# An attention kernel in float32: P·V as three products of split operands, and block 1's query blocks in rising order

## What is computed

```python
# block 1, two layers, 16 meta tokens ahead of the 1024; 8 heads of 64, one shared k and v
s = einsum('bqhd,bkd->bqhk', q_idx, k_idx)                  # index scores
score = einsum('bqhk,bqh->bqk', relu(s), w_idx * idx_scale)
score = where(visible, score, NEG_INF)
_, sel = lax.top_k(score, 256)                              # 256 keys per query
logits = einsum('bqhd,bqkd->bqhk', q, k[sel]) * attn_scale
p = softmax(where(valid, logits, NEG_INF))
attn = einsum('bqhk,bqkd->bqhd', p, v[sel])
y_a = einsum('bte,ed->btd', attn * silu(gate_a), w_a)
# block 2, one layer
y_na  = neighbourhood_attention(qa, ka, va, rpb) @ w_branch_na    # 8 heads, 8 x 16 window on a 16 x 64 grid
y_swa = windowed_gqa_with_sink(qb, kb, vb, sink) @ w_branch_swa   # 8 query heads, 2 kv heads, |i-j| <= 128
```

## Time and profile before

| | |
|---|---|
| median of 3 runs | 3604.36 us (3599.98 to 3604.37) |
| profiled execution | 3597.27 us, span 3595.4 us |
| TensorE busy | 3357.2 us, 93% |
| VectorE, ScalarE, GpSimd busy | 50%, 35%, 34% |
| mean granted TensorE clock | 0.973 |
| DMA | 230.59 MB, 64 GB/s |

### The profile page before, as it was taken

The page is one execution under the profiler, slowest core; times in us unless marked ns, Lnnn a source line. Parts: engine busy times, 40 slices in busy tenths (PEclk is TensorE's granted clock), DMA queues, the critical chain, the costliest instruction groups (busy, mean ns, idle before and its releaser), DMA issues. The chain is left out here.

```text
span 3595.4 us, 45087 instructions
## 1 busy us (share of the span) xinstructions
PE 3357.2 (93%) x18148; PEld 2932.0 (82%) x18148; DVE 1806.4 (50%) x3015; ACT 1261.4 (35%) x1894; POOL 1212.1 (34%) x835
## 2 busy tenths in 40 slices
PE   5899999998998999999898999998899899999997
PEld 4788999998888899999875788876777588888885
DVE  4578999653356799975424144433433411000014
ACT  4553212452265422135314344344522522222223
POOL 3324633215332363311434432311253432323331
PEclk8999999999999999999998999999999999999998
DMA  5101122204310112210322411111242111111111
GB/s 139 33 24 42 57 81 90 76 1 160 101 54 24 36 51 78 93 72 1 124 90 82 127 40 35 40 47 48 71 141 94 30 47 47 47 47 49 46 52 48
DMA packets 284175, 230.59 MB, mean 64 GB/s; under 512 B 31473, under 2 KB 257408, under 8 KB 283584
## 3 DMA queue, kind: packets, MB, share of 16 engines
q1 hardware_dynamic: 253792, 116.40, 12.0%
q0 software_dynamic: 23264, 85.89, 6.8%
q10 hardware_dynamic: 6912, 25.41, 1.8%
HBM read 177.29 MB, written 52.36 MB: 64 GB/s over the span
## 5 line engine op out<-in xcount | busy, mean ns | idle before, releaser
L548 PE MATMUL big<-H,wsp 128*128 128x348 f32 (+2 forms) x9792 | 1916.6, 355 | 70.6 <-POOL H L1605 33.9
L548 PEld LDWEIGHTS big<-H,wsp 128*128 128x128 f32 (+1 forms) x9792 | 1684.7, 190 | 271.8 <-issue 35.5
L1605 POOL TENSOR_TENSOR wsp<-raw,wsp 128x1024 fp32r<-128x1024 f32 (+2 forms) x246 | 544.0, 2211 | 1488.2 <-ACT wsp L1071 1478.1
L548 PE MATMUL big<-SP,wsp 128*128 128x512 f32 x1920 | 451.0, 395 | 0.0
L548 PEld LDWEIGHTS big<-SP,wsp 128*128 128x128 f32 x1920 | 359.1, 187 | 90.4 <-issue 1.7
L1071 ACT ACTIVATE wsp<-raw 128x1024 fp32r<-128x1024 f32 (+2 forms) x246 | 238.4, 969 | 509.0 <-PE big L548 372.0
L2263 DVE MAX8 top<-SC 128x8 f32<-128x272 f32 (+6 forms) x448 | 367.9, 821 | 0.0
L2269 DVE MATCH_REPLACE8 SC<-top,SC 128x272 f32<-128x272 f32 (+6 forms) x448 | 364.5, 814 | 0.0
L2422 DVE TENSOR_TENSOR X<-X,big 128x1024 f32<-128x1024 f32 (+1 forms) x26 | 29.6, 1139 | 476.1 <-PE big L548 475.9
L1119 ACT ACTIVATE rows_a<-rows_a,head_min 128x1040 f32<-128x1040 f32 (+8 forms) x130 | 101.9, 784 | 128.1 <-DVE head_min L2041 127.9
L697 PE MATMUL small<-V,PT_a 128*128 128x64 f32 x1152 | 146.4, 272 | 0.1
(11 more groups left out here) (268 smaller groups left out, 3828.3 us busy)
## 6 DMA issues: line engine op xcount, KB each, us to landing
raw<-in_w_in SPq DMA_DIRECT2D x108, 512.0 KB, 3.9
raw<-in_w_ff SPq DMA_DIRECT2D x64, 512.0 KB, 4.1
raw<-in_w_out SPq DMA_DIRECT2D x24, 512.0 KB, 5.3
gate_b_scratch<-tm POOLq DMA_DIRECT2D x16, 522.0 KB, 3.1
gate_a_scratch<-tm ACTq DMA_DIRECT2D x16, 522.0 KB, 2.9
tm<-gate_a_scratch POOLq DMA_DIRECT2D x16, 522.0 KB, 3.8
tm<-gate_b_scratch POOLq DMA_DIRECT2D x16, 522.0 KB, 4.6
tm<-xT_scratch POOLq DMA_DIRECT2D x16, 522.0 KB, 5.2
```

The costliest lines, as they stand in the source:

```text
L548: mm = pe.matmul(dst(o, width), w[wp][:, k, 0:cols], rhs(xp, k)[:, t0:t0 + width], start=(k == 0 and i == 0), stop=(k == rows - 1 and i == 2))
L1605: pool.tensor_tensor(dst, src, hi.bitcast(F32), ALU.subtract).then_inc(*S.inc(name, *key))
```

## The change

- P and V are split for their product. `V` and `V2` are float32r with a high and a low part; ScalarE copies the high part, VectorE subtracts for the low one (`values_lo`). `PT_a` and `PT_b` too: `move_hi` copies all tiles of a unit on ScalarE, `move_lo` subtracts on VectorE. `values` makes three products per tile: with P high those by both parts of V, for all tiles, then P low by V high.
- The transposes have two PSUM banks (`tiles_a`, `tiles_b`); where a unit has up to four tiles the banks alternate, else it is cut in two groups. Scores of 576 keys stand in one area of two banks, of which there is one instead of two; masks are one instruction each.
- TensorE makes the scores of unit k ahead of the transposes of k-2, VectorE the mask ahead of the move, and ScalarE the move of unit k-2 ahead of the exponent of unit k-1 (before: of unit k), and what runs beside (`between`) last.
- Block 1's query blocks run from 0 up to 7, with three row buffers in `tm`; silu gates are loaded block by block. The meta queries are left out in the last layer (`LAST_A`).
- The index stage leaves out query block 0, whose keys are all visible: `qi` has 896 columns in two pieces of 448.

```diff
+        V = sb("V", [P, 2, NQ, HD], F32R)
+        V_meta = sb("V_meta", [P, HD])
         SC = sb("SC", [P, SCORE_COLS])
...
-            for j in range(NQ - 1, -1, -1):
+            for j in range(NQ):
...
-        BLOCKS_A = [*range(NQ - 1, -1, -1), -1]
+        LAST_A = [-1] * (DEPTH - 1) + [NQ - 1]
+        BLOCKS_A = [*range(NQ), -1]
...
+        def tiles_a(u, k):
+            if u["tiles"] > 4:
+                return [(0, 0, 4), (1, 4, u["tiles"] - 4)]
+            return [(k % 2, 0, u["tiles"])]
...
+        def row_a(k):
+            return tm[:, (2, 3, 0)[k % 3], 0:1040]
...
+        def tiles_b(u, k):
+            if len(u["kts"]) > 4:
+                return [(0, 0, 3), (1, 3, len(u["kts"]) - 3)]
+            return [(k % 2, 0, len(u["kts"]))]
...
+        def logits_b(u, k):
+            at = k % 2 * BANK if u["key"][0] == "s" else 0
+            return big[0][:, at:at + u["n"]]
...
-                        pe.wait_ge(*S.at("masked", *units[k - 2]["key"]))
-                    near = min(u["n"], BANK)
+                    back = 2 if u["key"][0] == "s" else 1
+                    if k >= back:
+                        pe.wait_ge(*S.at("masked", *units[k - back]["key"]))
+                    at = logits_b(u, k)
                     for part in range(2):
...
                 def transposes(k):
                     u = units[k]
                     pe.wait_ge(*S.at("exped", *u["key"]))
-                    if k:
-                        for e in moved_events(units[k - 1]):
-                            pe.wait_ge(*S.at(*e))
-                    for kt, _, _ in u["kts"]:
-                        at = place(u, kt) * P
-                        mm = pe.transpose(big[1][:, at:at + P], rows_b[:, k % 4, kt * P:(kt + 1) * P], ident[:])
-                    mm.then_inc(*S.inc("turned", *u["key"]))
+                    for i, (bank, first, count) in enumerate(tiles_b(u, k)):
+                        if bank in bank_free:
+                            pe.wait_ge(*S.at(*bank_free[bank]))
+                        for kt in range(first, first + count):
+                            at = bank * BANK + (kt - first) * P
+                            mm = pe.transpose(big[1][:, at:at + P], rows_b[:, k % 4, kt * P:(kt + 1) * P], ident[:])
+                        mm.then_inc(*S.inc("turned", *u["key"], i))
...
                 def values(k):
                     u = units[k]
-                    for e in moved_events(u):
-                        pe.wait_ge(*S.at(*e))
                     if opens_b(u) and earlier_b(block_b(u)):
                         pe.wait_ge(*S.at("gated", *earlier_b(block_b(u))))
-                    at = column_b(u) * HD
-                    for i, (kt, rows, v) in enumerate(u["kts"]):
-                        mm = pe.matmul(small[slot_b(u)][:, at:at + HD], PT_b[0:rows, k % 2, kt, :], v,
-                                       start=(opens_b(u) and i == 0), stop=(closes_b(u) and i == len(u["kts"]) - 1),
-                                       skip_group_check=True)
+                    out = small[slot_b(u)][:, column_b(u) * HD:(column_b(u) + 1) * HD]
+                    n, total = 0, 3 * len(u["kts"])
+                    for name, of, parts in (("moved_hi", 0, (0, 1)), ("moved_lo", 1, (0,))):
+                        for i, (_, first, count) in enumerate(tiles_b(u, k)):
+                            pe.wait_ge(*S.at(name, *u["key"], i))
+                            for kt, rows, v in u["kts"][first:first + count]:
+                                for part in parts:
+                                    mm = pe.matmul(out, PT_b[0:rows, k % 2, of, kt, :], v[:, part, :],
+                                                   start=(opens_b(u) and n == 0), stop=(closes_b(u) and n == total - 1),
+                                                   skip_group_check=True)
+                                    n += 1
...
                             pe.wait_ge(*S.at(*e))
+                    if k < N:
+                        scores(k)
                     if 2 <= k < N + 2:
                         transposes(k - 2)
-                    if k < N:
-                        scores(k)
                     if k <= 3:
                         before(k)
                     if 3 <= k < N + 3:
...
+                        pe.wait_ge(*S.at("gated", "a", l, before_a(u["j"], 2)))
+                    out, first_of_bank = bank_a(u["j"])[:, u["h"] * HD:(u["h"] + 1) * HD], u["h"] == 0
+                    for name, of, parts in (("moved_hi", 0, (0, 1)), ("moved_lo", 1, (0,))):
+                        for i, (_, first, count) in enumerate(tiles_a(u, k)):
+                            pe.wait_ge(*S.at(name, *u["key"], i))
+                            for kt in range(first, first + count):
+                                for part in parts:
+                                    mm = pe.matmul(out, PT_a[:, k % 2, of, kt, :], V[:, part, kt, :],
+                                                   start=first_of_bank, stop=False, skip_group_check=True)
...
+                    if 3 <= k < N:
+                        scores(k)
                     if 2 <= k < N + 2:
                         turn(k - 2)
                         if units[k - 2]["h"] == HEADS - 1:
                             turn_meta(units[k - 2]["j"])
-                    if 3 <= k < N:
-                        scores(k)
                     if 3 <= k < N + 3:
...
-                free[0] = [("masked", "a", l, -1), ("gated", "a", l, -1)]
-                free[1] = [("moved_act", "a", l, -1), ("meta_moved", l, 0)]
+                free[0] = [("masked", *units[-1]["key"])]
+                free[1] = [*bank_free.values(), ("meta_moved", l, units[-1]["j"])]
+                if l < DEPTH - 1:
+                    pe.wait_ge(*S.at("masked", *units[-1]["key"]))
...
                                 claim(job, [emptied], 0)
-                            mm = products(job, hi_lo(H), pieces1, None, [k])
+                            mm = products(job, hi_lo(H), pieces_qi if c < 2 else pieces1, None, [k])
...
-        def act_attention(act, units, between=None):
+        def act_attention(act, units, between):
             N = len(units)
             for k in range(N + 5):
-                if between:
-                    between(k)
                 if 2 <= k < N + 2:
-                    move(act, units[k - 2], (k - 2) % 2, "act")
-                if k < N:
-                    u, at = units[k], column_b(units[k])
+                    move_hi(act, units[k - 2], k - 2, tiles_b, PT_b, weighted_before(units, k - 2))
+                if 1 <= k < N + 1:
+                    u, at = units[k - 1], column_b(units[k - 1])
...
+        def move_hi(act, u, k, tiles, PT, before):
+            for i, (bank, first, count) in enumerate(tiles(u, k)):
+                act.wait_ge(*S.at("turned", *u["key"], i))
+                if before is not None:
+                    act.wait_ge(*S.at("weighted", *before))
+                act.activation(PT[:, k % 2, 0, first:first + count, :], turned_tiles(bank, count), ACT.Copy)\
+                    .then_inc(*S.inc("moved_hi", *u["key"], i))
+        def move_lo(dve, u, k, tiles, PT, before):
+            for i, (bank, first, count) in enumerate(tiles(u, k)):
+                dve.wait_ge(*S.at("moved_hi", *u["key"], i))
+                if before is not None:
+                    dve.wait_ge(*S.at("weighted", *before))
+                dve.tensor_tensor(PT[:, k % 2, 1, first:first + count, :], turned_tiles(bank, count),
+                                  PT[:, k % 2, 0, first:first + count, :].bitcast(F32), ALU.subtract)\
+                    .then_inc(*S.inc("moved_lo", *u["key"], i))
...
-            ins.then_inc(*S.inc(f"moved_{who}", *u["key"]))
+                if 3 <= k < N + 1:
+                    exped(k - 1)
...
-                    if 2 <= k < N + 2:
-                        move(dve, units[k - 2], (k - 2) % 2, "dve")
                     if k < N:
                         masked(k)
+                    if 2 <= k < N + 2:
+                        move_lo(dve, units[k - 2], k - 2, tiles_b, PT_b, weighted_before(units, k - 2))
+                    if k == 3 and kind == "n":
+                        values_lo("nav", c)
...
+            def values_lo(what, c):
+                wait(("v_part", what, c))
+                dve.tensor_tensor(V2[:, 1, :, :], ps2(psum_of[("v", what, c)]).rearrange("p (k d) -> p k d", k=NQ),
+                                  V2[:, 0, :, :].bitcast(F32), ALU.subtract).then_inc(*S.inc("v_ready", what, c))
...
```

345 lines of the change are left out of this document (152 added, 193 removed).

## The result

The changed kernel takes **3887.8 us** (median of 4 runs, 3876.0 to 3903.8) against 3603.6 us for the kernel before in the same comparison: 1.0794 times as long, 95% interval 1.0751 to 1.0836. The direction was forecast, the size was not: 3728 us was written, 3775 the upper end, and the kernel lies 160 us above the forecast. The mean granted clock fell from 0.973 to 0.928.

What follows compares the result with a forecast made beforehand. TensorE, busy 93% of the span, was taken to bound the kernel. Terms 110 + 8 + 19 + 1 - 3 - 11 + 3 = +127 gave 3724 or 3731, written as 3728 us; range 3680 to 3775.

Steps and rivals of the forecast that it cites:

- P and V in two parts, +110: P·V in both blocks: three float32r loads replace two records per tile, 0.106 us more for each of 1040 tiles, +110 us.
- The two rivals that made loads cheaper: P·V: split products' loads hidden, 3585 us, 5%; or only the second product with the same P loads free, 3643, 6%.
- Switches, +8: Block 2's neighbourhood attention: 32 units visit their 64-key tile twice instead of once, 0.24 us each, +8 us (0 to 16).
- Starts, +19: Start of each neighbourhood pass: V ready later, 9.1 us against 4.3 to the first product, +19 over four passes (0 to 28).
- ScalarE's circle: Windowed attention: transposes, move, exponent form one circle, some 24 units pay 0.15 us; with products inside last-pass waits, together +1.
- block 1's order: Block 1: short units cost 16 us, 14 saved at the old end, 7 by the meta row, clock 2: -3 (-15 to +10).
- The rival of a longer circle: ScalarE's circle is 0.3 us longer and bounds units of four tiles and fewer, some 170 by 0.25 us: 3770 us, 14%.
- Index stage, -11: Index stage: leaving out query block 0 shortens product jobs and rotation, -11 us over both layers (-2 to -15).
- the meta row, -7: Block 1's last layer: loses its meta row, 6.96 us from the turn to the next stage's first product, counted as -7.
- Clock, +3 (0 to 12): New waits at the four neighbourhood pass starts may call up the 1.2 GHz clock, +3 us, from 0 to 12.

Runs made afterwards that it cites:

- filled: Changed kernel with products nobody reads (14 and 18) put in TensorE's pauses at the start of each neighbourhood pass; 3776.4 us, 1.0486 against the kernel before.
- two_products: Changed kernel without the third product of each tile (P's low part by V's high part); 3768.3 us, 1.0468 against the kernel before.
- full_rows: Changed kernel with the fifth, 64-key tile of a neighbourhood unit multiplied over all 128 rows; 3872.0 us, 1.0741 against the kernel before.
- no_split: Changed kernel with one fp32 product per tile in all attentions, everything else as in the change; 3663.2 us, 1.0173 against the kernel before.
- filled_stall: Changed kernel with start pauses filled, plus 56 tiny ScalarE copies ahead of unit 4's move in each neighbourhood pass; 3886.9 us, 1.0788 against the kernel before.
- before_late_v: Kernel before, with ScalarE's between-unit work (V's bias and copy) put behind the unit's own work in neighbourhood passes; 3660.6 us, 1.0161 against the kernel before.

## Why the prediction was right on the sign and wrong on the size

- **P and V in two parts, +110.** Right. The spacing is 0.11 us a load (21 in 2.42 us), three loads a tile, none spared. 29 and 27 us a layer in block 1 for 30.5; in "filled" a neighbourhood pass's P·V stretch grows by 10.8 us for 7.6 and 2 for the switches. In two_products two of the three products of a tile cost block 1 what the float32 product does, 156 us for 155 a layer. The two rivals that made loads cheaper fall.
- **Switches, +8.** Right: full_rows shortens a pass's P·V stretch by 4.1 to 4.4 us, half of whose visits are new, so 8 to 9 over four passes, at the low clock that they ran at.
- **Starts, +19.** Right as a wait: 10.2 us against 9.1, the two waits 2.5 and 3.6 where 2.9 and near 4 were named. By the starts of the stages it is 5.5 to 6.4 a pass, 25 in all. But the same 19 us were also the trigger, and that is the next point.
- **ScalarE's circle and block 1's order, +1 and -3.** Too low. In no_split block 1's P·V stretches are 12 us longer a layer (up to 5 of it the clock) and begin 6 to 7 us sooner behind the first scores, so the order costs 11 to 13 us where the sum had 4. The windowed passes have 6 more than the sum, the clock left aside. The rival of a longer circle had this sign; at its 0.25 for all short units it is not what happened.
- **Index stage, -11, and the meta row, -7.** The first is -11.3 by the stages; alone it gave 15.8 between the medians (interval of the ratio 10 to 21). The meta row gave 3 and not 7: the sum counted the last block's turning back and splitting as part of it, and they stay.
- **Clock, +3 (0 to 12): the step that failed.** The rows named showed a low clock beside waits, and I took the clock to be low while TensorE waits, and the price to be some us of dip. What the runs show is that the clock stays at 1.2 GHz for 61 to 85 us of almost unbroken work behind a pause. Closing the pauses (filled) gives 111 us back; opening one in the repaired kernel (filled_stall) takes 110. With 10 to 11 us for the stretch of 51 in the last windowed pass (P·V stretch 44.3 against 32.8 to 34.1 in the passes before it), that is some 122 us where 3 stood. In that last pass no new pause was needed: its waits were there before, with 7 us at 1.2 GHz behind them, and the split products made 51 of it. The term had no place for that either, since it tied the clock to the four new waits alone. Every low stretch in the trace before is 17 us or shorter, so nothing in it pointed beyond the 12 of the range; that no neighbourhood pass there began with a wait over 1 us was to be seen too, and the change put pauses of 2.5 and 3.6 into all four. I had priced the pauses and not asked what the work behind them would run at.

Sum check, by the profiled executions: 127 forecast, + 4 in block 1, + 4 for the meta row, + 2 in the other stages ahead of block 2, + 124 in the neighbourhood passes (114 of them clock), + 17 in the windowed ones (11 clock), + 1 behind them = 279; they differ by 278.7.

What stays open is what sets the length of a low stretch. The products have a part: 51 us against 7 behind like waits in the last windowed pass; in the neighbourhood passes split 58 to 89 us, with 128 columns 20 to 51, and fp32 with somewhat shorter waits 10 in no_split and 7 to 48 in before_late_v. The place has a part: the long stretches end in the 12th unit of a pass or behind it. The rest varies with the execution: in block 1 it is 10 to 68 us behind pauses of 4.7 and 6.0. No run tells what the rule is.
